# Chunk 0 ahead of chunk 1 around the three normalizations of a decoder layer

## The reference, cut to what matters

```
def ffn_half_step(x, w1, w3, w2, g, b):
    return layer_norm(ALPHA * x + 0.5 * swiglu(x, w1, w3, w2), g, b)
...
hp = ffn_half_step(xp, ffn1_w1[l], ffn1_w3[l], ffn1_w2[l], ln1_g[l], ln1_b[l])
...
xp = layer_norm(ALPHA * hp + mp, ln2_g[l], ln2_b[l])
...
xp = ffn_half_step(xp, ffn2_w1[l], ffn2_w3[l], ffn2_w2[l], ln3_g[l], ln3_b[l])
```

## Time and profile before

| | |
|---|---|
| median of 3 runs | 1151.06 us (1150.54 to 1152.31) |
| profiled execution, its own time | 1150.81 us |
| its span, first to last instruction | 1149.0 us |
| PE busy | 1125.8 us, 98% |
| DVE busy | 553.2 us, 48% |
| ACT busy | 376.0 us, 33% |
| POOL busy | 149.4 us, 13% |
| mean granted clock of PE | 0.996 of full speed |

### The profile page before, as it was taken

The page is one execution under the profiler, slowest core; times in us unless marked ns, Lnnn a source line. Parts: engine busy times, 40 slices in busy tenths (PEclk is TensorE's granted clock), DMA queues, the critical chain, the costliest instruction groups (busy, mean ns, idle before and its releaser), DMA issues.

```text
span 1149.0 us, 21803 instructions
## 1 busy us (share of the span) xinstructions
PE 1125.8 (98%) x8774; PEld 1100.5 (96%) x8774; DVE 553.2 (48%) x960; ACT 376.0 (33%) x677; POOL 149.4 (13%) x171
## 2 busy tenths in 40 slices
PE   7999999999999999999999999999999999999996
PEld 7999999999999989998899999799999999999994
DVE  3443433243443475887545556944442233435346
ACT  5222222222223334375542234522231222223334
POOL 2000000000001426900000025140000000000240
PEclk9999999999999999999999999999999999999998
DMA  9322441233233143221132332232342223334102
GB/s 251 94 82 83 134 129 56 74 92 92 85 114 95 56 130 74 83 65 38 47 92 83 102 98 69 62 105 81 90 127 80 64 74 92 91 95 134 29 1 78
DMA packets 191991, 101.15 MB, mean 88 GB/s; under 512 B 15209, under 2 KB 189533, under 8 KB 191896
## 3 DMA queue, kind: packets, MB, share of 16 engines
q1 hardware_dynamic: 189712, 95.77, 29.2%
q0 software_dynamic: 2208, 4.38, 1.2%
HBM read 97.63 MB, written 3.68 MB: 88 GB/s over the span
## 4 chain that ended last, share of the span: by engine, by line
PE 90%; DVE 6%; ACT 2%; issue 1%; DMA 0%; SPq 0%; DVEq 0%; ACTq 0%
PE psum L1222 29%; PE psum L1220 29%; PE psum L1221 29%; DVE y L916 1%; DVE act_lo L923 1%; DVE ring_lo L836 1%; DVE y L897 1%; DVE stat L902 1%; PE psum L1423 1%; PE psum L1439 1%; DMA xin<-in_x_prompt 0%; PE psum L1456 0%; DVE y L861 0%; PE psum L1350 0%; ACT ring_hi L558 0%
## 5 line engine op out<-in xcount | busy, mean ns | idle before, releaser
L1220 PE MATMUL psum<-act_hi,ring_hi 128*128 128x272 f32 x1824 | 531.0, 291 | 6.2 <-DVE act_lo L923 3.6
L1222 PE MATMUL psum<-act_hi,ring_lo 128*128 128x272 f32 x1824 | 529.0, 290 | 0.0
L1221 PE MATMUL psum<-act_lo,ring_hi 128*128 128x272 f32 x1824 | 525.6, 288 | 0.0
L1220 PEld LDWEIGHTS psum<-act_hi,ring_hi 128*128 128x128 f32 x1824 | 344.3, 189 | 14.9 <-DVE act_lo L923 6.0
L1221 PEld LDWEIGHTS psum<-act_lo,ring_hi 128*128 128x128 f32 x1824 | 345.0, 189 | 0.0
L1222 PEld LDWEIGHTS psum<-act_hi,ring_lo 128*128 128x128 f32 x1824 | 344.0, 189 | 0.0
L836 DVE TENSOR_TENSOR ring_lo<-raw,ring_hi 128x1024 fp32r<-128x1024 f32 (+1 forms) x169 | 200.4, 1187 | 297.9 <-ACT ring_hi L558 251.6
L558 ACT ACTIVATE ring_hi<-raw 128x1024 fp32r<-128x1024 f32 (+1 forms) x169 | 171.3, 1015 | 230.3 <-PE psum L1222 230.0
L598 ACT ACTIVATE tmp_a<-psum 128x272 f32<-128x272 f32 x184 | 73.1, 397 | 419.6 <-PE psum L1222 357.8
L1220 PE MATMUL psum<-hid_hi,ring_hi 128*128 128x272 f32 x512 | 148.6, 290 | 0.0
L1221 PE MATMUL psum<-hid_lo,ring_hi 128*128 128x272 f32 x512 | 147.0, 287 | 0.0
(11 more groups left out here) (185 smaller groups left out, 1167.1 us busy)
## 6 DMA issues: line engine op xcount, KB each, us to landing
raw<-in_ffn_w SPq DMA_DIRECT2D x175, 256.0 KB, 3.2
raw<-in_ffn_w SPq DMA_DIRECT2D x32, 512.0 KB, 4.0
raw<-in_w_in SPq DMA_DIRECT2D x52, 256.0 KB, 3.3
ext_raw<-in_ffn_w SPq DMA_DIRECT2D x32, 192.0 KB, 4.1
raw<-in_w_out SPq DMA_DIRECT2D x16, 256.0 KB, 3.2
raw<-in_w_pool_out SPq DMA_DIRECT2D x16, 128.0 KB, 2.3
raw<-in_w_attn_out SPq DMA_DIRECT2D x16, 128.0 KB, 2.8
xin<-in_x_prompt SPq DMA_DIRECT2D x6, 256.0 KB, 5.1
```

The costliest lines, as they stand in the source:

```text
L1220: pe.matmul(o, weights(s, k, True), x_hi[:, k, tok(c)], start=k == 0, stop=False)
L1221: pe.matmul(o, weights(s, k, True), x_lo[:, k, tok(c)], start=False, stop=False)
L1222: ins = pe.matmul(o, weights(s, k, False), x_hi[:, k, tok(c)], start=False, stop=k == kn - 1)
```

## The change

There are five edits. They are taken together here.

- **Down products of the second half of both FFNs** follow `DOWN_ORDER`: chunk 0 runs five units ahead, so that (7,0) is done before (3,1). `stats` of chunk 0 sit inside part (3,1), before its eighth tile. DVE takes variance, center and reciprocal around the residual of (3,1). Units 6 and 7 need weights beside the ring: `far_hi`, `far_lo`, and a dead part of `act_lo`.
- **Scaling in pieces**: in FFN 1 chunk 0 is scaled in four pieces (`SCALE_PIECES`) behind the residuals of (4,1) to (7,1); in FFN 2 it is scaled behind (4,1), with ACT's part in three pieces (`LAST_PIECES`).
- **Output product chunk by chunk** (`WO_ORDER`): all eight parts of chunk 0, then all eight of chunk 1. Its units 4 to 7 and FFN 2's first two units have slots of their own (`spare`: `out_w`, `att_lo`, `att_hi`, `near_w`); chunk 1 rotates over banks 0 to 3. DVE adds from PSUM directly (`residual_out`), without ACT's copy. Chunk 0 is scaled in two large instructions (`norm_ratio`), ACT makes `act_hi` and the final `y` (`norm_both`, which also takes the place of POOL's `add_bias` for chunk 0), and DVE subtracts two tiles at a time (`norm_low`).
- **`stats` of chunk 1** follow the next product's first part instead of preceding it; `poolctx` and `kctx` follow unit 3 of the mixer.
- **Weight splits** stand earlier by a step: unit 3 at the start before `turned(TURNS0)`, and those around the normalizations by `DOWN_SPLITS`, `NEXT_SPLITS`, `WO_SPLITS`.

```
+DOWN_ORDER = [(0, 0), (1, 0), (2, 0), (0, 1), (3, 0), (1, 1), (4, 0), (2, 1), (5, 0), (6, 0), (7, 0), (3, 1), (4, 1),
+              (5, 1), (6, 1), (7, 1)]
+DOWN_SPLITS = {(0, 1): [4], (1, 1): [5], (4, 0): [6], (2, 1): [7]}
+NEXT_SPLITS = {(5, 1): [8], (6, 1): [9], (7, 1): [10]}
+SCALE_PIECES = {(4, 1): (0, 3), (5, 1): (3, 6), (6, 1): (6, 8), (7, 1): (8, 10)}
+LAST_PIECES = {(4, 1): (0, 2), (5, 1): (2, 5), (6, 1): (5, 8)}
+WO_ORDER = [(s, c) for c in range(2) for s in range(DOWN)]
+WO_SPLITS = {(0, 0): [5], (1, 0): [6], (2, 0): [7], (3, 0): [8], (4, 0): [9], (5, 1): [10], (6, 1): [11]}
+WO_AFFINE = {(2, 1): (0, 2), (3, 1): (2, 4), (4, 1): (4, 6), (5, 1): (6, 8)}
+WO_LOW = {(4, 1): (0, 1), (5, 1): (1, 2), (6, 1): (2, 4)}
...
+            def residual_out(u, c, o):
+                dve.wait_ge(mm_done[c], u + 1)
+                dve.wait_ge(evac[c], u)
+                dve.scalar_tensor_tensor(out=y[:, o, tok(c)], in0=y[:, o, tok(c)], scalar=ALPHA,
+                                         in1=psum[:, bank_of(u, c), 0:C], op0=ALU.mult, op1=ALU.add) \
+                    .then_inc(evac[c], 1)
...
+                    for s, c in DOWN_ORDER if half == 1 else ():
+                        if (s, c) == (3, 1):
+                            norm_var(l, 0)
+                        residual(b + s, c, s, 1.0)
+                        deviation(l, c, s)
+                        if (s, c) == (3, 1):
                             norm_center(l, 0)
+                            norm_reciprocal(l, 0)
+                        for n in DOWN_SPLITS.get((s, c), ()):
+                            split(b + n, KF)
+                        if l == 2 and (s, c) == (4, 1):
+                            norm_scale(l, 0)
+                        nexts = NEXT_SPLITS.get((s, c), ()) if l == 0 else ()
+                        for n in nexts if s < DOWN - 1 else ():
+                            split(b + n, KD)
+                        if l == 0 and (s, c) in SCALE_PIECES:
+                            norm_scale(l, 0, *SCALE_PIECES[s, c])
+                        for n in nexts if s == DOWN - 1 else ():
+                            split(b + n, KD)
...
             split(2, KD)
+            split(3, KD)
             turned(TURNS0)
-            split(3, KD)
...
+            split(WO_BASE + 4, KD)
+            for s, c in WO_ORDER:
+                if s == 0:
+                    dve.wait_ge(biased[c], KD)
+                if (s, c) == (1, 1):
+                    norm_var(1, 0)
                     norm_center(1, 0)
+                residual_out(WO_BASE + s, c, s)
+                deviation(1, c, s)
+                if (s, c) == (1, 1):
+                    norm_reciprocal(1, 0)
+                if (s, c) == (2, 1):
+                    norm_ratio(0)
+                if (s, c) in WO_LOW:
+                    norm_low(0, *WO_LOW[s, c])
+                for n in WO_SPLITS.get((s, c), ()):
+                    split(WO_BASE + n, KD)
...
+                if at is None and c and WO_BASE + 2 <= u < FFN2_BASE:
+                    pe.wait_ge(evac[0], min(u + 5, FFN2_BASE))
+                    pe.wait_ge(evac[1], u - 3)
...
                 for k in range(kn):
+                    if inside and k == inside[0]:
+                        inside[1]()
...
+            for s, c in WO_ORDER:
+                part(WO_BASE + s, c, KD, m_hi, m_lo, ready=m_wait(c) if s == 0 else None,
+                     inside=(6, lambda: stats(1, 0)) if (s, c) == (0, 1) else None)
```

More of the change, by code:

```diff
@@ L470, in all_norm_sums @@
             def all_norm_sums(l):
-                for s in range(DOWN + LAG):
-                    norm_sums(l, 0, s)
-                    norm_sums(l, 1, s - LAG)
+                for s, c in WO_ORDER if l == 1 else DOWN_ORDER:
+                    norm_sums(l, c, s)
             pool.wait_ge(mm_done[0], UP)
@@ L483, in add_bias @@
                 pool.wait_ge(act_ready[1], KD * (l + 1))
-                for c in range(2):
+                for c in (1,) if l == 1 else range(2):
                     pool.wait_ge(act_ready[c], KD * (l + 1))
@@ L895, in norm_center @@
                 dve.tensor_tensor(s, psum[:, bank ^ 1, 0:C], s, ALU.subtract).then_inc(var_done[c], 1)
-                for half in halves:
+            def norm_center(l, c):
+                bank = stat_bank(l, c)
+                mean = psum[:, bank:bank + 1, 0:C].broadcast_to([P, 4, C])
+                for i in range(2):
+                    half = y[:, 4 * i:4 * i + 4, tok(c)]
                     ins = dve.tensor_tensor(half, half, mean, ALU.subtract)
@@ L913, in norm_scale @@
                     return
-                for o in range(KD + 2):
+                for o in range(lo, hi):
                     if o < KD:
@@ L1307, in hid_wait @@
                         return lambda k: pe.wait_ge(hid_done[c], hid_n + k + 1)
-                    for s in range(DOWN + LAG):
-                        if l == 0 and half == 0 and s == 1:
+                    for s in range(DOWN + LAG) if half == 0 else ():
+                        if l == 0 and s == 1:
                             pe.wait_ge(vecs_done, 1)
```

262 lines of the change are left out of this document (156 added, 106 removed).

## The result

The changed kernel takes **1149.55 us** (median of 20 runs, 1148.08 to 1151.57) against 1151.51 for the kernel before on the same chips: a ratio of 0.9984, 95% interval 0.9977 to 0.999. The forecast was 1138.9 us with a range of 1135 to 1144; the gain is 2 us where 12.2 were expected. The profiled execution has a span of 1147.9 us, against 1149.0.

A forecast was written before the change was run, and what follows sets the result against it. PE, busy for 98% of the span, was taken as the bound, with at most 17.3 us of its waits removable. Terms -3.8 - 7.0 - 1.2 - 0.2 = -12.2 us took 1151.06 to 1138.9 us, range 1135 to 1144.

The forecast's parts named there:

- the ledger of DVE's chain behind FFN 1: Timed DVE's work from the end of part (3,1) to chunk 0's last `act_lo` at 21.9 us, 2.7 late.
- FFN 1 to mixer, -3.8: Between FFN 1's down products and mixer part (4,0): 7.2 us of stall would shrink to 3.4.
- one op slowed: In DVE's work behind part (3,1): one instruction slowed by POOL, 1.02 us against 0.44.
- the split for (4,0): Before mixer part (4,0): no longer behind ACT's copies of cached rows, so 0.1 us of its 0.64 is left.
- The clock: Mixer to FFN 2, at 722 to 727: low granted clock after PE starved, about 1.7 of 7.9 us of stall.
- rival 2: FFN 1 hand-over gains nothing (+3.8), PE may fall to 1.2 GHz (+1.7): 1142.7 to 1144.4 us; chance 0.18.
- Output product, "it keeps up": Output product, chunk 0: DVE's 0.5, 0.4 and 1.2 us of work fit each part of 3.01 us.
- Mixer to FFN 2, -7.0: From the output product's end to FFN 2's part (4,0): 7.9 us of stall would shrink to 0.9.
- The end, -1.2: End of the kernel: chunk 1's variance starts with the end of `stats`, 1.2 us earlier, all of it gained.
- The start, -0.2: Start: unit 3's earlier weights gain 0.2 us, between 0 and 1.0, since (0,1) still waits for ACT's copies.
- The chance of 0.92 for "faster": Whole kernel: chance that the change makes it faster, summed from 0.70, 0.18 and 0.04.

The follow-up runs named there:

- e3_narrow: The changed kernel with POOL's sums of the first layer norm over 8 columns instead of 272, for pricing only: 1142.93 us.
- e4_psum: The changed kernel with DVE adding the residual straight from PSUM in both FFNs' second down products, without ACT's copy: 1144.49 us.
- e7_old: The changed kernel with the end of the first FFN put back as before on all engines, the rest kept: 1147.08 us.
- e10_before: The kernel before, unchanged, profiled a second time: 1151.03 us in one execution.
- e2_busy: The changed kernel with 32 extra matmuls into an unused bank inside the mixer's first chunk-0 part, where PE stands still: 1146.89 us.
- e5_wo: The changed kernel with ACT making the next weights' high part ahead of its norm work in the output product's chunk-0 steps: 1148.45 us.
- e8_all: The changed kernel with residual from PSUM, ACT's splits first in the output product, 34 filler matmuls at the end, DVE's last splits behind chunk 0's low parts: 1137.98 us.

## Why the prediction was wrong

The step that failed first and most is the ledger of DVE's chain behind FFN 1: it has one instruction slowed by POOL, where six groups were, and it follows the stall that it leaves without the clock behind it. By terms:

- **FFN 1 to mixer, -3.8: came out as +1.0 to +1.5, a miss of about 5 us.** The order of events was right: DVE is behind PE, the stall sits in the first part, at inner blocks 4 and 6. Wrong was the size of DVE's chain. The ledger has "one op slowed"; e3_narrow shows six groups slowed, 3.55 us, of which the ledger had 0.58. The chain ended at 24.4 and not at 21.9, so 2.5 us of the miss are this, and most of the rest is the clock of the next point. The ACT hand-overs were in it at 0.5 each; they were right, but e4_psum shows that they could be avoided. And where the prediction says that the split for (4,0) is worth 0.5, e7_old shows 0.8.
- **The clock.** The prediction priced it at 722, where PE "had been starved", as 1.7 of the 7.9 us of stall. That price was wrong: in e10_before the clock is 1.00 there and the stretch as long, 27.77 us. It changes no sum, since the whole 7.9 were to go, but it puts the cost at the wrong place. What the clock would do behind the stall that the prediction's own ledger leaves in the mixer's first part it asked only in rival 2. e2_busy prices it at 1.8 to 2.3 us.
- **Output product, "it keeps up": +1.4.** DVE's load per part was right, 2.1 us of 3.0. The step left out the engine ahead of it: ACT's wait for the shift (2.77), copy and table load (1.28) stand ahead of one high half, squares ahead of the next, and DVE waits, in order, with the residual behind it. e5_wo shows it whole.
- **Mixer to FFN 2, -7.0: -5.1.** The clock is 1.00 now, which by itself gave nothing. Of the 0.9 us that should have been left there are 2.8, since 22.67 less 19.9 is 2.8. ACT's affines come every 0.51 us and not every 0.42. DVE's pairs of `act_lo` (L1002) took 1.25 each at 721.51 and not 0.66, while POOL was adding again (721.20 and 722.18); the like pairs of L1183, elsewhere in the kernel, took 0.72, and the one pair of the same kind that POOL left alone, in e8_all, 0.73. It is the error of FFN 1 a second time. With DVE's splits behind the low parts the stretch is 21.10.
- **The end, -1.2: nothing.** The mechanism is in the trace, variance right behind the statistics. It was taken back twice: 0.67 us by ACT's copy behind the affine pieces, which I had listed for FFN 1 and not looked for in FFN 2, and 0.5 us by the clock, as the transposes go from 4.5 us to 5.04 (the kernel before ran them from 1138.45 to 1143.0).
- **The start, -0.2:** zero.
- **The rivals.** Rival 2 had the whole mechanism of FFN 1 (four or five instructions more slowed, no gain there, the fall of the clock inside a part) at 0.18. It gives that hand-over 3.8 + 1.7 = 5.5 us more than the forecast, and 4.8 to 5.3 were measured. It treats the three other losses as if they were none, and so its time, 1142.7 to 1144.4, is 5 us too low too. The chance of 0.92 for "faster" counted a sum in which every term had the same sign. Three of the four terms, and the nothing that it puts for the output product, rested on DVE and ACT keeping a schedule with no slack, and their errors all go one way.

The losses add up: 4.8 (mixer), 1.4, 1.9 (FFN 2), 1.4 (end), 0.2 and 0.3 (down products) make 10.0 of the 10.65 us between 1138.9 and 1149.55. Of the rest, 0.45 is that the forecast started from a median of 1151.06 for the kernel before, and twenty executions gave 1151.51.

## What to carry to other kernels

When a change spreads one engine's chain into the gaps of others, price each instruction by what runs beside it at its new time, not at its old one, and follow the engine ahead of it in program order as far as the engine itself. A stall that is split or moved is worth its own length plus, where PE then sets the pace, the clock behind it. So ask of each stall that a plan leaves what the granted clock did behind the like of it, and whether PE or another engine is the bound there; a few matmuls without use can be cheaper than the fall. One profile is too few to price a fall of the clock: the one at 722 came in one of two. And when the terms of a sum all rest on the same schedule, their errors are not independent: the range must be much wider than that of one of them.
